# Two down projections by one step of Strassen's algorithm with 512 moving columns, and the exponents of gated attention by one-pass products

## Chip, cores and metric

One core of a Trainium2 chip runs a two-layer transformer trunk in one launch. The metric is the device time of that core in microseconds (us); lower is better.

## What is computed

The trunk runs on 1024 prompt tokens and, with the same weights, on 64 sample tokens (8 sequences of 8), all in float32. Layer 0 mixes by gated linear attention and sparse attention, layer 1 by sliding-window attention with sinks; each is followed by a gated feed-forward block. Cut to what matters here:

```python
def trunk(x, ...):
    for l in range(2):
        mix = even_or_odd_mixing(l, x)
        h = layer_norm(ALPHA * x + mix, ln_g[l, 0], ln_b[l, 0])
        x = layer_norm(ALPHA * h + swiglu(h, ffn_w_gu[l], ffn_w_down[l]), ln_g[l, 1], ln_b[l, 1])

def swiglu(h, w_gu, w_down):          # w_gu 1024 x 5632, w_down 2816 x 1024
    g, u = split(h @ w_gu)
    return (silu(g) * u) @ w_down     # the down projection
```

Gated linear attention works in chunks of tokens. Of each chunk it needs exp(sum of log gates / 16) for many sets of summands; these sums are products of the log gates z (128 tokens x 256 features) with constant 0/1 matrices `sums`.

## The kernel before

**Splits.** Where float32 precision is wanted at one pass of TensorE, an operand is split in two F32R tensors: `hi = round(x)` (ScalarE copy) and `lo = x - hi` (VectorE, or GpSimd in the input projections). A product is then three matmuls: hi hi, lo hi and hi lo. Where a tensor is used as plain F32, TensorE takes each matmul in more passes; the trace has two records for each of them.

**`ffn_up`** (from L2091) makes the gated activations by Strassen-Winograd with moving operands of 272 columns and stores them in DRAM (`a_dram`, 22 blocks of 128 features x 1088 tokens).

**`ffn_down`** (from L2387) computes 1088 tokens x 2816 x 1024 and the second layer norm of the layer, once per layer (tags `ffn0d` and `ffn1d`). The 1024 output columns go in 4 chunks of 256 (`NF`). For chunks 0 to 2 the loop over the 22 feature blocks is outside and the 9 token tiles (8 of 128, one of 64 sample tokens) inside, so that 9 tiles x 3 matmuls use one pair of splits (L2475); all tiles of a chunk accumulate in PSUM, two to a bank. The last chunk goes tile by tile (L2507), so that each tile is finished and normalised while the next is multiplied. The moving operand is always the weight block of 256 columns, the stationary one 128 (or 64) tokens of the activations. In all 4 x 22 x 9 x 3 = 2376 matmuls.

- SyncE (L2435 on) loads weights in a ring of 8 buffers and each activation block `aT[:, k, :]` once.
- ScalarE makes `w_hi` (256 columns) and `a_hi` (1088), L2523 and L2552, in the last chunk groups of up to 1024 columns (L2529).
- VectorE makes `w_lo` (L2593) and `a_lo` (L2616, L2600), adds each chunk to the residual `X` (`add`, L2587), and does the layer norm's statistics, centre and reciprocal (L2049 to L2075).
- GpSimd loads `X` and adds the norm's bias (L2080). It does nothing else in this stage.
- With `XT` given (layer 0) each finished tile is transposed by TensorE (L2491) and copied by ScalarE (L2535) for the next stage.

ScalarE waits for the last activations of `ffn_up` before it starts, since the split buffers take the place of that stage's buffers.

**Gated attention** (second Block of `even_in`) runs beside the last three chunks of the input projection. For each chunk i of 128 tokens (8 prompt chunks, then the samples) there are 8 levels l. The order of TensorE's work is written out by hand: at each level some units of the projection (`LEVEL_UNITS`; 6 matmuls of 256 columns each), at levels 0 to 2 a preparatory step for the next chunk, then `level(i, l)`, and at levels 3 to 7 one of five parts of `exponents(i + 1)` (L698): `z` of 128 features stationary, two of nine `sums` matrices (256 columns) moving, both plain F32. `level(i, l)` waits until VectorE has taken level l - 1 (`take_level`, L1006), and each part of `exponents` until ScalarE has exponentiated the part before (L855). VectorE's order at level 1 is: take the level, `late_scaled(i)` (L997, L998), `clip(i + 1)` (L977), `mean_square`. `qk_transposes` (L707) waits for `clip`. ScalarE at level 1: `gates`, then `inverse_rms` with its reload of the exponential's table, and only then, at level 2, `qk_copies`.

## Time and profile before

| | |
|---|---|
| median of 3 runs | 3362.34 us (3362.22 to 3362.91) |
| the profiled execution | 3366.61 us |
| its span, first to last instruction | 3364.9 us |
| mean granted TensorE clock | 0.942 of full speed |
| TensorE busy with matmuls | 3046.8 us, 91% |
| VectorE, ScalarE, GpSimd busy | 49%, 38%, 23% |
| DMA | 241.14 MB, mean 72 GB/s |

A busy TensorE is not TensorE at its peak: matmuls overlap, so what one costs is the distance from its start to the next one's start, not the duration in its record. The idle time before an instruction stands in brackets with what ended it.

### The profile page before, as it was taken

What the parts mean: (1) busy time and instruction counts of PE and PEld (TensorE: products, weight loads), DVE (VectorE), ACT (ScalarE), POOL (GpSimd) and SP (SyncE); (2) the same over time, 40 slices, a digit from 0 to 9 for tenths busy, and PEclk for the clock granted to TensorE, in tenths of its full rate; (3) what the DMA queues carried; (4) which work ended last, traced back from release to release, by engine and by line L of the source; (5) the groups of instructions that cost most, each with busy time, mean ns of one, the idle gap of its engine ahead of it and who ended that gap; (6) DMA issues with size and microseconds to landing.
All of it is one profiled execution on the core that took longest, in us unless ns stands there. A gap on an engine that the chain in (4) does not pass through costs nothing. (4 is left out here: it accounts for less than half of the span.)

```text
span 3364.9 us, 56085 instructions
## 1 busy us (share of the span) xinstructions
PE 3046.8 (91%) x21594; PEld 2653.5 (79%) x21613; DVE 1648.0 (49%) x3148; ACT 1267.7 (38%) x2701; POOL 759.5 (23%) x917
## 2 busy tenths in 40 slices
PE   7999998678999789999999969869996999999997
PEld 7888776354665489999999869836665999999997
DVE  2166343574898363333355634325546333334566
ACT  2222443333565443333344432114444333333343
POOL 2200221530121034444200014400002444430002
PEclk8999997798999899999999989969998999999999
DMA  4201102533100122222351112130002222217111
GB/s 129 76 27 42 26 26 79 161 87 121 35 30 28 44 66 73 81 77 77 127 174 51 41 57 39 64 109 23 32 20 70 77 78 77 78 53 266 38 54 54
DMA packets 253632, 241.14 MB, mean 72 GB/s; under 512 B 55635, under 2 KB 213542, under 8 KB 253350
## 3 DMA queue, kind: packets, MB, share of 16 engines
q1 hardware_dynamic: 244630, 217.87, 21.1%
q0 software_dynamic: 8752, 19.81, 1.9%
q8 instruction: 172, 2.82, 0.4%
q14 instruction: 78, 0.64, 0.1%
HBM read 183.46 MB, written 55.89 MB: 71 GB/s over the span
## 5 line engine op out<-in xcount | busy, mean ns | idle before, releaser
L2204 PE MATMUL ffn0u_ps<-ffn0u_x_hi,ffn0u_whi 128*128 128x272 f32 x1232 | 359.2, 292 | 19.8 <-DVE ffn0u_wlo L2307 11.1
L2204 PE MATMUL ffn1u_ps<-ffn1u_x_hi,ffn1u_whi 128*128 128x272 f32 x1232 | 358.7, 291 | 19.3 <-DVE ffn1u_wlo L2307 10.8
L2204 PE MATMUL ffn0u_ps<-ffn0u_x_hi,ffn0u_wlo 128*128 128x272 f32 x1232 | 356.7, 290 | 0.0
L2204 PE MATMUL ffn1u_ps<-ffn1u_x_hi,ffn1u_wlo 128*128 128x272 f32 x1232 | 356.6, 289 | 0.0
L221 PE MATMUL ine_ps<-ine_w_hi,ine_x_hi 128*128 128x256 f32 (+2 forms) x864 | 261.2, 302 | 5.1 <-DVE ine_w_lo L237 5.0
L2204 PEld LDWEIGHTS ffn0u_ps<-ffn0u_x_hi,ffn0u_whi 128*128 128x128 f32 x1232 | 234.8, 191 | 22.1 <-DVE ffn0u_wlo L2307 20.6
L2204 PEld LDWEIGHTS ffn1u_ps<-ffn1u_x_hi,ffn1u_whi 128*128 128x128 f32 x1232 | 234.5, 190 | 21.6 <-DVE ffn1u_wlo L2307 20.2
L221 PE MATMUL ine_ps<-ine_w_hi,ine_x_lo 128*128 128x256 f32 (+2 forms) x864 | 245.3, 284 | 0.0
L221 PE MATMUL ine_ps<-ine_w_lo,ine_x_hi 128*128 128x256 f32 (+2 forms) x864 | 244.7, 283 | 0.0
L2204 PEld LDWEIGHTS ffn0u_ps<-ffn0u_x_hi,ffn0u_wlo 128*128 128x128 f32 x1232 | 235.0, 191 | 0.0
L2204 PEld LDWEIGHTS ffn1u_ps<-ffn1u_x_hi,ffn1u_wlo 128*128 128x128 f32 x1232 | 234.6, 190 | 0.0
L2204 PE MATMUL ffn1u_ps<-ffn1u_q,ffn1u_whi 128*128 128x272 f32 x704 | 202.5, 288 | 0.0
L2204 PE MATMUL ffn0u_ps<-ffn0u_q,ffn0u_whi 128*128 128x272 f32 x704 | 202.5, 288 | 0.0
L2475 PE MATMUL ffn1d_ps<-ffn1d_w_hi,ffn1d_a_hi 128*128 128x256 f32 (+1 forms) x594 | 171.1, 288 | 14.9 <-DVE ffn1d_a_lo L2609 7.8
L2475 PE MATMUL ffn0d_ps<-ffn0d_w_hi,ffn0d_a_hi 128*128 128x256 f32 (+1 forms) x594 | 171.2, 288 | 14.6 <-DVE ffn0d_a_lo L2609 7.5
L221 PEld LDWEIGHTS ine_ps<-ine_w_hi,ine_x_hi 128*128 128x128 f32 (+1 forms) x864 | 161.8, 187 | 16.1 <-issue 8.3
L2475 PE MATMUL ffn1d_ps<-ffn1d_w_hi,ffn1d_a_lo 128*128 128x256 f32 (+1 forms) x594 | 170.1, 286 | 0.0
L2475 PE MATMUL ffn1d_ps<-ffn1d_w_lo,ffn1d_a_hi 128*128 128x256 f32 (+1 forms) x594 | 170.0, 286 | 0.0
L2475 PE MATMUL ffn0d_ps<-ffn0d_w_hi,ffn0d_a_lo 128*128 128x256 f32 (+1 forms) x594 | 169.8, 286 | 0.0
L2475 PE MATMUL ffn0d_ps<-ffn0d_w_lo,ffn0d_a_hi 128*128 128x256 f32 (+1 forms) x594 | 169.7, 286 | 0.0
L221 PEld LDWEIGHTS ine_ps<-ine_w_hi,ine_x_lo 128*128 128x128 f32 (+1 forms) x864 | 161.9, 187 | 4.8 <-issue 4.0
L221 PEld LDWEIGHTS ine_ps<-ine_w_lo,ine_x_hi 128*128 128x128 f32 (+1 forms) x864 | 161.9, 187 | 0.0
(537 smaller groups left out, 8279.2 us busy)
## 6 DMA issues: line engine op xcount, KB each, us to landing
aT<-scratch_a SPq DMA_DIRECT2D x42, 544.0 KB, 7.6
ffn0u_raw<-in_ffn_w_gu_dram SPq DMA_DIRECT2D x44, 512.0 KB, 5.2
ffn1u_raw<-in_ffn_w_gu_dram SPq DMA_DIRECT2D x44, 512.0 KB, 5.5
scratch_a<-ffn0u_u SPq DMA_DIRECT2D x44, 272.0 KB, 2.1
scratch_a<-ffn1u_u SPq DMA_DIRECT2D x44, 272.0 KB, 2.1
ffn0d_w<-in_ffn_w_down_dram SPq DMA_DIRECT2D x88, 128.0 KB, 2.5
ffn1d_w<-in_ffn_w_down_dram SPq DMA_DIRECT2D x88, 128.0 KB, 2.5
ine_w<-in_w_in_even_dram SPq DMA_DIRECT2D x5, 1024.0 KB, 5.4
```

Source lines behind the costliest of these rows:

```text
L221: last = nc.tensor.matmul(o, xp[:, k, i * P:i * P + r], wp[:, g % RING, 0:n], start=(k == 0 and j == 0 and i % 2 == 0), stop=(k == KD - 1 ...
L2204: last = nc.tensor.matmul(ps[:, bank + h, 0:TOK2], wp, xp, start=(begins and k == 0 and n == 0), stop=(k == KH - 1 and n == 2), skip_group ...
L2475: last = nc.tensor.matmul(acc(i), ap[:, n % 2, i * P:i * P + rows(i)], wp[:, k, :], start=(k == 0 and j == 0 and i % 2 == 0), stop=(k == K ...
```

## The change

**Down projection.** `ffn_down` is rewritten. Activations A (1024 prompt tokens x 2816) and weights B (2816 x 1024) are each cut in 2 x 2 quadrants; seven products of half-size factors, with 11 feature blocks each, replace eight. In a product each of 11 steps multiplies 4 tiles of 128 tokens with a weight block of 512 columns: 12 matmuls a step. Factors that are sums are made on the way: all 55 sums of weights on GpSimd, and of the 55 sums of activations 37 on GpSimd and 18 on VectorE (`dve_sums_a`), each of 128x512. The splits are now two blocks of 128x512 per step, in rings of 5. The 64 sample tokens ride beside products 0, 1, 4 and 5: their hi and lo parts lie side by side as one stationary operand of 128 columns, so two matmuls a step do, and a `fold` matmul adds the halves. Each product is added to one or two quadrants of `X` by VectorE (`take`, 48 additions of 128x512) at step 3 of the next product. Weights come in a ring of 3 (plus 2 for second summands). The norms of tiles 0 to 3 are made within products 5 and 6, those of the samples and tiles 4 to 7 after the last step's splits; the last three steps of product 6 go tile by tile.

```diff
-def ffn_down(nc, st, A, l, tag, aT, XT, y_out, a_out, place=None):
-    NCH, NB, RAW, AG = D // NF, (TILES + 1) // 2, 8, 8
+def ffn_down(nc, st, A, l, tag, aT, XT, y_out, a_out):
+    KH2, HT, HN, RB, RW, RS, TAIL = KF // 2, SEQ // 2, D // 2, 5, 3, 2, 3
+    FACTOR_A = [(A11,), (A11, ADD, A12), (A11, ADD, A22), (A12, SUB, A22), (A22,), (A21, ADD, A22), (A21, SUB, A11)]
+    FACTOR_B = [(B12, SUB, B22), (B22,), (B11, ADD, B22), (B21, ADD, B22), (B21, SUB, B11), (B11,), (B11, ADD, B12)]
+    INTO = [[(0, 1, ADD), (1, 1, ADD)], [(0, 0, SUB), (0, 1, ADD)], [(0, 0, ADD), (1, 1, ADD)], [(0, 0, ADD)],
+            [(0, 0, ADD), (1, 0, ADD)], [(1, 0, ADD), (1, 1, SUB)], [(1, 1, ADD)]]
+    def dve_sums_a(n):
+        return n in a_sum_at and n in w_sum_at and n % KH2 % 2 == 0
...
             @block.sync
...
+                    if n in raw_at:
+                        r = raw_at[n]
+                        if r >= RW:
+                            sp.wait_ge(w_split, raw_steps[r - RW] + 1)
...
             @block.tensor
...
+                def tile_step(p, k, t):
+                    n = p * KH2 + k
+                    for j, (ap, wp) in enumerate(((a_hi, w_hi), (a_lo, w_hi), (a_hi, w_lo))):
+                        last = nc.tensor.matmul(ps[:, bank(p, t), :], ap[:, n % RB, t * P:t * P + P], wp[:, n % RB, :],
+                                                start=(k == 0 and j == 0), stop=(k == KH2 - 1 and j == 2), skip_group_check=True)
...
             @block.scalar
...
+                def split(n):
+                    if n in w_sum_at:
+                        act.wait_ge(w_sum_done, w_sum_at[n] + 1)
...
+                    if n >= RB:
+                        act.wait_ge(step_done, n - RB + 1)
+                    nc.scalar.copy(w_hi[:, n % RB, :], w_source(n)).then_inc(w_hi_done, 1)
...
+                    nc.scalar.copy(a_hi[:, n % RB, :], a_source(n)).then_inc(a_hi_done, 1)
...
             @block.gpsimd
...
+                for n in range(STEPS):
+                    if n in w_sum_at:
+                        sum_w(pool, nc.gpsimd, n)
+                    if n in a_sum_at and not dve_sums_a(n):
+                        sum_a(pool, nc.gpsimd, n, a_sum_pool)
...
             @block.vector
...
+                for n in range(STEPS):
+                    if n + 1 < STEPS and dve_sums_a(n + 1):
+                        sum_a(dve, nc.vector, n + 1, a_sum_dve)
+                    dve.wait_ge(w_hi_done, n + 1)
+                    nc.vector.tensor_tensor(w_lo[:, n % RB, :], w_source(n), w_hi[:, n % RB, :].bitcast(F32),
                                             ALU.subtract).then_inc(w_split, 1)
+                    dve.wait_ge(a_hi_done, n + 1)
+                    nc.vector.tensor_tensor(a_lo[:, n % RB, :], a_source(n), a_hi[:, n % RB, :].bitcast(F32),
+                                            ALU.subtract).then_inc(a_split, 1)
...
+                    if p >= 1 and k == 3:
+                        take_all(p - 1)
...
+                norm(3)
+                ln.dve_rstd(dve, 3)
+                for i in range(4, NT):
+                    half_stats(i, 0)
+                add_sample(0)
+                norm(NT)
+                ln.dve_rstd(dve, NT)
+                for t in range(4):
+                    take(NPROD - 1, t)
+                    half_stats(4 + t, 1)
+                    ln.dve_center(dve, 4 + t, link)
+                    ln.dve_rstd(dve, 4 + t)
```

`sum_a` waits until the low part of the sum two before it has been made (`RS` = 2).

**Gated attention.** `z` is split too, by two operations of VectorE in `log_gates`; the `sums` are copied to F32R once at the start; each part of `exponents` is now two F32R matmuls (`z_hi`, `z_lo`) for each 128 features in place of one F32 matmul. `late_scaled` moves behind `clip` and `mean_square`. On ScalarE `qk_copies` comes before the reload of the exponential's table. For the samples, the levels are interleaved with the products with the old state, and the last norm is made between the updates of the states.

```diff
-                        which = sums_p[:, a:b, :] if i < NT else sums_s[:, a:b, :]
                         for p in range(2):
-                            last = nc.tensor.matmul(exponents_of(i, a, b)[:, :, p, :], z[0:r, p * P:(p + 1) * P], which,
-                                                    start=True, stop=True)
+                            for part in (z_hi, z_lo):
+                                last = nc.tensor.matmul(exponents_of(i, a, b)[:, :, p, :], part[0:r, p * P:(p + 1) * P], which,
+                                                        start=part is z_hi, stop=part is z_lo)
...
                         if l == 1:
-                            late_scaled(i)
                             clip(i + 1)
                             if i >= 1:
                                 mean_square(i - 1)
+                            late_scaled(i)
```

## Rows read from the trace of the kernel before

**Rows 1.** The page, part 1: busy time, share of the span, instructions.

```profile
PE 3046.8 (91%) x21594; PEld 2653.5 (79%) x21613; DVE 1648.0 (49%) x3148; ACT 1267.7 (38%) x2701; POOL 759.5 (23%) x917
```

**Rows 2.** Lines L2475, L2507: durations ns (min/median/max), first and last start us.

```profile
L2475 PE MATMUL ffn0d_ps<-ffn0d_w_hi,ffn0d_a_hi x594: 277/283/552, 1663.7 to 1891.2; 128*128 128x256 f32 x198
L2475 PE MATMUL ffn1d_ps<-ffn1d_w_hi,ffn1d_a_hi x594: 277/283/553, 3043.6 to 3271.3; 128*128 128x256 f32 x198
...
L2507 PE MATMUL ffn0d_ps<-ffn0d_w_lo,ffn0d_a_hi x198: 276/283/415, 1891.8 to 1992.9; 128*128 128x256 f32 x176, 128*64 128x256 f32 x22
L2507 PE MATMUL ffn1d_ps<-ffn1d_w_lo,ffn1d_a_hi x198: 277/283/283, 3271.9 to 3351.6; 128*128 128x256 f32 x176, 128*64 128x256 f32 x22
```

**Rows 3.** Timeline, PE, 256 columns: start, duration; 24 rows left out.

```profile
3340.51 0.28 PE L2507 MATMUL ffn1d_ps<-ffn1d_w_hi,ffn1d_a_lo 128*128 128x256 f32 x1
...
3343.51 0.28 PE L2507 MATMUL ffn1d_ps<-ffn1d_w_lo,ffn1d_a_hi 128*128 128x256 f32 x1
```

**Rows 4.** Timeline, PEld, before F32 matmuls of 512 columns; 3 rows left out.

```profile
2300.22 0.19 PEld L2989 LDWEIGHTS odd_ps<-odd_w,odd_YT 128*128 128x128 f32 x1 [0.24 <-issue]
...
2301.94 0.19 PEld L2989 LDWEIGHTS odd_ps<-odd_w,odd_YT 128*128 128x128 f32 x1 [0.24 <-issue]
```

**Rows 5.** Timeline of POOL, then DVE, in the up projection.

```profile
2701.77 1.30 POOL L2155 TENSOR_TENSOR ffn1u_wlo_full<-ffn1u_raw,ffn1u_wlo_full 128x512 f32<-128x512 f32 x1
2703.01 1.80 POOL L2155 TENSOR_TENSOR ffn1u_wlo_full<-ffn1u_raw 128x512 f32<-128x512 f32 x1
2704.78 1.74 POOL L2155 TENSOR_TENSOR ffn1u_wlo_full<-ffn1u_raw,ffn1u_wlo_full 128x512 f32<-128x512 f32 x1
...
2702.97 2.39 DVE L2307 TENSOR_TENSOR ffn1u_wlo<-ffn1u_raw,ffn1u_whi 128x512 fp32r<-128x512 f32 x2 [3.51 <-ACT ffn1u_whi L2216]
2705.28 0.77 DVE L2322 TENSOR_TENSOR ffn1u_x<-ffn1u_x,ffn1u_ps 128x272 f32<-128x272 f32 x2
```

**Rows 6.** Groups by line, ACT, 2550 to 3043 us: busy us, mean ns.

```profile
L2216 ACT CAST ffn1u_whi<-ffn1u_wlo_full 128x512 fp32r<-128x512 f32 x88 | 52.4, 617 | 7.9 <-POOL ffn1u_wlo_full L2155 7.9
```

**Rows 7.** Stretches: length, busy PE, PEld, DVE, ACT, POOL, granted clock, DMA share, GB/s.

```profile
1920.00:1950.00 30.00, 23.96 (x168) 23.54 (x168) 14.75 (x25) 9.89 (x14) 4.80 (x2) 0.84 0.09 36
...
3043.00:3070.00 27.00, 26.37 (x198) 26.41 (x199) 12.97 (x17) 11.55 (x17) 0.00 (x0) 0.87 0.99 374
```

**Rows 8.** Timeline, PE: the first matmul of the down projection.

```profile
3043.63 0.55 PE L2475 MATMUL ffn1d_ps<-ffn1d_w_hi,ffn1d_a_hi 128*128 128x256 f32 x1 [7.78 <-DVE ffn1d_a_lo L2609]
```

**Rows 9.** Timeline of DVE, ACT, POOL: the norm of the last tiles, both layers.

```profile
3345.09 0.41 DVE L2587 SCALAR_TENSOR_TENSOR ffn1d_X<-ffn1d_X,ffn1d_ps 128x256 f32<-128x256 f32 x1
...
3346.58 1.28 DVE L2058 SCALAR_TENSOR_TENSOR ffn1d_X<-ffn1d_X,ffn1d_ln_mv,ffn1d_ln_gb 128x1024 f32<-128x1024 f32 x1
3347.77 0.16 DVE L2075 RECIPROCAL ffn1d_ln_rstd<-ffn1d_ln_rstd 128x1 f32<-128x1 f32 x1
...
3354.78 2.19 ACT L2070 ACTIVATE ffn1d_X<-ffn1d_X,ffn1d_ln_rstd 128x1024 f32<-128x1024 f32 x2 [1.12 <-DVE ffn1d_ln_rstd L2075]
...
3356.01 4.64 POOL L2080 TENSOR_TENSOR ffn1d_X<-ffn1d_X,ffn1d_ln_gb 128x1024 f32<-128x1024 f32 x2 [4.37 <-ACT ffn1d_X L2070]
...
2002.83 0.80 ACT L2535 COPY XT_odd<-ffn0d_ps 128x256 f32<-128x256 f32 x2 [0.44 <-PE ffn0d_ps L2491]
```

**Rows 10.** What PE waited for, 325 to 600 us: total, times, longest us.

```profile
PE ine_ps L707 <- DVE gla_z L977: 12.4, 8, 2.4
```

**Rows 11.** Timeline of PE and DVE in gated attention, prompt chunks.

```profile
380.18 1.13 PE L698 MATMUL ine_ps<-gla_sums,gla_z 128*128 128x256 f32 x4
380.96 0.47 PE L221 MATMUL ine_ps<-ine_w_hi,ine_x_hi 128*128 128x256 f32 x1
...
387.66 0.49 PE L747 MATMUL ine_ps<-H,gla_A 128*128 128x128 f32 x2
...
386.83 0.77 DVE L1006 COPY_PREDICATED gla_A<-ine_lev,ine_ps 128x256 f32<-128x256 uint8 x2 [0.93 <-PE ine_ps L727]
...
400.70 1.22 DVE L997 TENSOR_TENSOR gla_E<-gla_E,gla_KQ 128x1024 f32<-128x1024 f32 x1
```

More of the change, by code:

```diff
@@ L793, in _ @@
                 kin_transposes(NT)
-                for l in range(1, lv(NT)):
-                    level(NT, l)
-                pe.wait_ge(lev_used, lev0[NT + 1])
+                level(NT, 1)
                 pe.wait_ge(late_done, NT + 1)
+                pe.wait_ge(late_evac, NB * (NCH - CW))
                 pe.wait_ge(ss_in, 32)
@@ L920, in _ @@
                 kin_copy(NT)
+                log_mean_square(NT - 1)
                 inverse_rms(NT - 1)
@@ L2030, with __init__ @@
 class LayerNorm:
-    def __init__(self, st, ctx, tag, l, which, X, A):
+    def __init__(self, st, ctx, tag, l, which, X, A, order=tuple(range(TILES))):
         nc = st.nc
+        self.pos = {i: n for n, i in enumerate(order)}
         self.nc, self.X = nc, X
@@ L2437, in ffn_down, with sum_a, bank @@
+        def sum_a(eng, op, n, done):
+            u, k = a_sum_at[n], n % KH2
+            x, sign, y = FACTOR_A[n // KH2]
+            wait_block(eng, x, k)
+            wait_block(eng, y, k)
+            if u >= RS:
+                eng.wait_ge(a_split, a_sum_steps[u - RS] + 1)
+            op.tensor_tensor(a_sum[:, u % RS, :], a_block(x, k), a_block(y, k), sign).then_inc(done, 1)
+        def bank(p, t):
+            return (4 * p + t) % 7
         with nc.Block() as block:
@@ L2512, in _ @@
+                for t in range(4):
+                    for k in range(KH2 - TAIL, KH2):
+                        last = tile_step(NPROD - 1, k, t)
+                    last.then_inc(tile_done, 1)
+                    if XT is not None and t < 3:
+                        transposes((2, 3, NT)[t])
                 if XT is not None:
-                    for i in range(TILES - 3, TILES):
+                    for i in range(4, NT):
                         transposes(i)
@@ L2579, in _ @@
+                for i in NORM_ORDER[2:]:
                     ln.pool(pool, i)
@@ new lines, in take @@
+                def take(p, t):
+                    if t < 3 or p == NPROD - 1:
+                        dve.wait_ge(tile_done, 3 * p + t + 1)
+                    else:
+                        dve.wait_ge(step_done, KH2 * (p + 1))
+                    for h, c, sign in INTO[p]:
+                        if p == 0 and h == 0:
+                            dve.wait_ge(*((x_first, 32) if t == 0 else (x_right, 32)))
+                        elif p == 1 and t == 0 and c == 0:
+                            dve.wait_ge(x_left0, 16)
+                        elif p == 4 and t == 0 and h == 1:
+                            dve.wait_ge(x_left1, 16)
+                        add((p, t, h, c), 4 * h + t, c, sign, ps[:, bank(p, t), :])
@@ new lines, in take_all, with add_sample, half_stats, norm @@
+                def take_all(p):
+                    for t in range(4):
+                        take(p, t)
+                def add_sample(c):
+                    dve.wait_ge(s_folded, 2 - c)
+                    if c == 1:
+                        dve.wait_ge(x_sample, 16)
+                    add(("s", c), NT, c, ADD, ps[0:NS, S_BANK, :])
+                def half_stats(i, c):
+                    dve.wait_ge(added, touched[(i, c)])
+                    ln.dve_half_stats(i, c, link)
+                def norm(i):
+                    half_stats(i, 0)
+                    half_stats(i, 1)
+                    ln.dve_center(dve, i, link)
@@ new lines, in sample_lo @@
+                def sample_lo(n, slot, src):
+                    dve.wait_ge(s_hi, n)
+                    nc.vector.tensor_tensor(s_a[:, slot, :, NS:2 * NS], src, s_a[:, slot, :, 0:NS].bitcast(F32),
+                                            ALU.subtract).then_inc(s_lo, 1)
+                nc.vector.tensor_tensor(fold[:, :], st.ident[:, 0:NS], st.ident[:, NS:P], ALU.add).then_inc(fold_made, 1)
+                for n in range(STEPS):
+                    if n + 1 < STEPS and dve_sums_a(n + 1):
+                        sum_a(dve, nc.vector, n + 1, a_sum_dve)
@@ new lines, in _ @@
+                    p, k = divmod(n, KH2)
+                    if n == 0:
+                        sample_lo(1, 0, aT[:, 0:KH2, SEQ:NTOK])
+                    elif n == 8:
+                        for h in range(2):
+                            dve.wait_ge(s_in[h], 16)
+                        nc.vector.tensor_tensor(s_sum[:, :, :], aT[:, 0:KH2, SEQ:NTOK], aT[:, KH2:KF, SEQ:NTOK],
+                                                ALU.add).then_inc(s_summed, 1)
+                    elif n == 10:
+                        sample_lo(2, 1, s_sum[:, :, :])
+                    elif n == 2 * KH2:
+                        sample_lo(3, 0, aT[:, KH2:KF, SEQ:NTOK])
```

538 lines of the change are left out of this document (311 added, 227 removed).

## The prediction

> **What bounds the kernel now.** I read the page's busy times first: TensorE works 91% of the span [rows 1], so a stage gets shorter where its matmuls get fewer or cheaper, as long as what feeds them keeps up. Next, per line, where the down projections lie: their matmuls run from 1663.7 to 1993.2 us in layer 0 and from 3043.6 to 3351.9 us in layer 1 [rows 2], 329.5 and 308.3 us. Then the timeline, for what a matmul costs: 25 steps of 256 columns in 3.00 us, 120 ns each [rows 3]. Here 2376 x 0.120 = 285 us of each projection is plain TensorE work; the other engines have slack. After the last matmul the norm of the last tiles remains: layer 1's span ends at 3364.9, layer 0's last copy at 2003.6 [rows 9]. The two projections so take 321.3 us (3043.6 to 3364.9) and 339.9 us (1663.7 to 2003.6). Layer 0 is slower since its last chunk also transposes tiles and stalls, in part at a granted clock of 0.84 [rows 7].
>
> **1. Price of a 512-column matmul.** The count falls from 2376 x 256 columns to 7 x 11 x 12 = 924 for the prompt and 4 x 11 x 2 = 88 for the samples, 1012 x 512. No F32R matmul of 512 columns is in the trace. 512 columns take 213.3 ns at 2.4 GHz, 256 take 106.7. At 256 the steps are 13 ns longer than the columns [rows 3]; at 512, in plain F32 with two rounds of columns to a record, 4 steps take 1.72 us, 430 ns, only 3 over 2 x 213.3 [rows 4]. So the price lies between 214 and 226 ns. I take 216, the row with the same number of columns, since there too one weight load hides behind twice its own columns. 1012 x 0.216 = 218.6; two folds in F32, two records of 0.43 each, 1.7; start at the lower clock as now, 13% of 27 us [rows 7], 3.5. TensorE alone: **224 us**.
>
> A rule of the Trainium skill (TensorE: Matmul & The Clock Gate, section Back-to-back issue gap) gives N/2.4 + 2.5 ns for an isolated matmul, 215.8 at 512, but names about 131 ns as the sustained figure at N = 512. The same formula gives 109 ns at 256, where this trace has 120; by 131 ns the sum would be 133 us instead of 219.
>
> **2. What feeds it: VectorE and GpSimd take turns.** GpSimd has 55 + 37 = 92 sums of 128x512 per layer, VectorE 154 low parts + 18 sums. The timeline of the up projection shows the two together [rows 5]. Alone, a GpSimd sum is followed by the next after 1.24 us (2701.77 to 2703.01). The next one meets a low part of VectorE and is followed only after 1.77 (to 2704.78), and VectorE's two low parts last 2.39 us. GpSimd and VectorE do not overlap there: one sum and one low part cost 1.24 + 0.53. VectorE's operations with a PSUM operand (0.77 for two, at 2705.28) run beside GpSimd at their usual pace, so the 48 additions of `take` don't count in this. By product:
> - 0, 1, 4, 5: 11 x 1.24 + 22 x 0.53 = 25.3 us, against TensorE's 11 x 14 x 0.216 = 33.3 us. Hidden.
> - 2, 3, 6: 16 x 1.24 + 28 x 0.53 = **34.7 us**, against 11 x 12 x 0.216 = 28.5 us. Not hidden: 6.2 us short each, plus about 1.5 for moments in which neither has work.
>
> The rings give credit. ScalarE may split step n once step n - 5 is done; its two copies take 0.62 each [rows 6], the low part 0.6, so a step is ready 4 x 2.59 - 1.9 = 8.5 us ahead. Products 2 and 3 together need 2 x 7.7 = 15.4, so 7 us of stall. Products 4 and 5 restore the credit (`take_all`, 8 additions of 0.68, 5.4 us in which no low part is made, fits in it; 0.68 is estimated from the 0.41 of 256 columns [rows 9] and 0.27, half of the 0.53 above). Product 6 needs 7.7, and one norm addition on GpSimd (2.3) and a centre (1.2) fall on it: 11.2 - 8.5, some 4 with holes. **11 us** of stalls per layer, and 4 for the clock when TensorE idles in short pieces, of which half the loss seen at 0.84 [rows 7] is my measure (0.16 x 30 = 4.8).
>
> The Trainium skill (SBUF — State Buffer, section SBUF: two separate sides) calls this an exclusive lock on a port pair that both use, held for the whole instruction; it holds for VectorE operations with two SBUF inputs. By that rule, the trace agrees.
>
> **3. Start.** Now the first matmul comes 7.78 us late [rows 8]. The new chain has 512 weight columns, not 256, and a GpSimd sum of 1.24 us before the high part, but that sum waits for nothing of ScalarE. I add 1.
>
> **4. Tail.** The last 36 matmuls (7.8 us) can only begin once the splits of the last step are made, and so does the chain of norms. Per tile of 128 the centre holds the shared turn for 1.2, GpSimd's bias 2.3 (4.64 for two), and they alternate: reciprocal, ScalarE's scale 1.1 (2.19 for two), GpSimd 2.3 to 2.4, centre of the next tile 1.2 [rows 9]. That is 4.8 us per tile, though VectorE's own sequence from addition to reciprocal takes 2.75 (3345.09 to 3347.84) [rows 9]. Chain after the last split: norm of tile 3 (the 2.75 without an addition but with both halves' statistics, 0.7 each by the 1.49 from addition to centre [rows 9]: 3.3), four half statistics and the samples' addition (3.6), the samples' norm (3.2), addition and statistics of tile 4 and its wait for GpSimd's turn with the samples (4.7), four centres at 4.8 distance (14.4), scale, bias and store of the last (1.1 + 2.4 + 4.2, the last from the end of GpSimd at 3360.65 to the end of the span). Sum 37 us for layer 1. In layer 0, 33 to the last bias and 2.3 for transposes and copies.
>
> **5. Sum of the projections.** Layer 1: 1 + 224 + 11 + 4 - 7.8 + 37 = 269.2, against 321.3: -52. Layer 0: 1 + 224 + 15 - 7.8 + 2 (transposes within the stage) + 33 + 2.3 = 269.5, against 339.9: -70. TensorE's own saving of about 60 us is thus partly given back in layer 1 by stalls and a longer tail, while layer 0 also loses its present stalls.
>
> **6. Gated attention.** Four records of `exponents` and the way to the next projection matmul take 380.18 to 380.96 and the 0.19 us that this one starts early (0.47 against 0.28): 0.97 us [rows 11]. Four F32R matmuls of 256 columns are 4 x 0.12 = 0.48. For the parts at levels 3 to 5 that is 1.5 us per chunk. At levels 6 and 7 I count nothing: there TensorE is already level with VectorE's `take_level` (0.77 us from 386.83, the outputs at 387.66) [rows 11], which would be late next. `clip` no longer stands behind `late_scaled`, whose first operation alone lasts 1.22 [rows 11]; TensorE's wait for it is 12.4 us over 8 chunks [rows 10], 1.5 each, and goes. The two new operations of VectorE on `z` (about 0.4 each) make `exponents` wait some 0.3. `qk_copies` a table load earlier is off the path. Net 2.7 x 8 = 21.6, and 2 for the samples' reordering: **-23**. The sums' conversion and two more small tensors hide behind the 16 units of projection at the start.
>
> **Total:** 52 + 70 + 23 = 145 us. The profiled execution took 3366.6 us, 4.3 above the median; off the median 3362.3 the forecast is **3217 us**. A measurement of this kernel can tell about 0.2%, 7 us, from no change.
>
> **The rivals.**
> - *No turn-taking to speak of*: short waits interleave, TensorE is never starved, and the tail goes at VectorE's 2.75 to 3.0 us per tile. Then 2 x (15 + 8) less: 3171. Against it: 1.77 against 1.24 [rows 5].
> - *512 columns at 226 ns*, the excess of [rows 3] kept: 2 x 10 more, of which the stalls absorb a part: 3229 to 3237.
> - *The feed loop is slower than the turns.* With 3 weight buffers, low part to load to GpSimd's sum to high part to low part must go round once in three steps, and a_sum has two buffers. If steps of products 2, 3 and 6 take 3.8 us instead of 3.3: 2 x 33 x 0.5 = 33 more, 3250.
> - *Gated attention gives nothing*, since level and `take_level` alternate anyway: 3240.
> - *The other sign: slower.* Place: VectorE's queue in `ffn_down`. If each of its 172 low parts and sums had to wait for one whole GpSimd operation, 172 x 1.77 + 48 x 0.68 = 337 us per layer in place of 239, so 3217 + 196 = 3413. It decides from 145/2/172 = 0.42 us of extra waiting per operation. Against it: GpSimd has just 92 operations to be waited for.
> - *TensorE stops binding*: matmuls of 512 columns overlap so far that the turns alone set the pace, 4 x 25.3 + 3 x 34.7 = 205 us in place of 239, 34 less per layer: 3149. Nothing in the rows points there; 256 columns already cost 120 ns [rows 3]. The sustained figure of the Trainium skill's TensorE page (above) would lead here.
>
> **Chances.** Forecast 42%, no turn-taking 15%, 226 ns 13%, slower loop 16%, attention nothing 9%, slower 3%, TensorE not binding 2%. The range reaches from the first rival to the third with some room for sums of them: 3172 to 3255. All but one case are faster by over 0.2%: faster 0.96, same 0.01, slower 0.03.
>
> **What would show it.** Right: steps of 216 ns within product 0; in products 2, 3 and 6 steps of about 3.2 us with TensorE waiting for `w_lo` or `a_lo`, GpSimd sums lasting 1.8 where VectorE is busy; last matmul about 22 us (layer 1) before the span's end, against 13 now; no wait at the `qk` transposes. Wrong: TensorE waiting in product 0 or 1 (a DMA or ring bound), or 512-column steps over 230 ns, or GpSimd sums at 1.3 throughout.

## The result, and the profile after it

The changed kernel takes **3269.22 us** (median of 6 runs, 3264.14 to 3282.22), beside 3362.62 us for the kernel before (6 runs, 3361.39 to 3370.67): ratio 0.9722, 95% interval 0.9706 to 0.9737. That is faster, as forecast, but 52 us above the forecast of 3217 and 14 us above the upper end of the range. The profiled execution took 3274.2 us (span 3272.5), 5 above the median.

The page of the changed kernel, part 1 (busy time, share of the span, instructions), answers to [rows 1]:

```profile
PE 2939.8 (90%) x18874; PEld 2460.4 (75%) x18893; DVE 1775.2 (54%) x3186; ACT 1204.3 (37%) x2655; POOL 1040.3 (32%) x1097
```

VectorE has 127 us more to do and GpSimd 281 more; TensorE is busy for 107 less. To find where the time went, I read in both traces when the first matmul of each stage starts and took differences (us):

| part | before | after | difference | predicted |
|---|---|---|---|---|
| input projection with gated attention | 586.5 | 583.0 | -3.5 | -23 |
| the up projection ahead of layer 0's down projection, with the wait at its start | 490.4 | 493.4 | +3.0 | +1 |
| layer 0: its first matmul to the next stage's | 350.3 | 293.2 | -57.1 | -71 |
| the same ahead of layer 1's | 489.9 | 491.9 | +2.0 | +1 |
| layer 1: its first matmul to the end of the span | 321.3 | 285.8 | -35.5 | -53 |
| all other stages | | | -1.2 | 0 |
| sum | | | -92.3 | -145 |

Three parts fall short of the forecast: the attention by 19.5 us, layer 0 by 16 and layer 1 by 18.5, the starts included.

**The matmuls.** Timeline of TensorE in product 2 of layer 1 (start, duration; it answers to [rows 3]):

```profile
3066.21 0.39 PE L2604 MATMUL ffn1d_ps<-ffn1d_w_hi,ffn1d_a_hi 128*128 128x512 f32 x1
...
3069.85 0.39 PE L2604 MATMUL ffn1d_ps<-ffn1d_w_hi,ffn1d_a_lo 128*128 128x512 f32 x1
```

From the first to the second, 16 matmuls start in 3.64 us: 227.5 ns for 512 columns. Over the 213.3 ns (512 / 2.4) that the prediction counts for the columns, the excess is 14 ns, as it was 13 at 256 [rows 3].

**The waits.** What TensorE waited for in layer 1, 2985 to 3273 us (total, times, longest):

```profile
PE ffn1d_ps L2604 <- DVE ffn1d_X L2780: 11.7, 2, 6.5
PE ffn1d_ps L2604 <- DVE ffn1d_a_lo L2828: 10.8, 2, 9.9
PE ffn1d_ps L2604 <- DVE ffn1d_X L2776: 1.9, 1, 1.9
```

The 9.9 is the start (7.8 before [rows 8]). Apart from that, TensorE hardly waits for the low parts, where the prediction had put its stalls. It waits for lines L2780 and L2776, the additions of `take`. The timeline around the longest of these waits, at the change from product 2 to product 3, TensorE first, then VectorE:

```profile
3096.47 0.39 PE L2604 MATMUL ffn1d_ps<-ffn1d_w_lo,ffn1d_a_hi 128*128 128x512 f32 x1
3103.36 0.80 PE L2604 MATMUL ffn1d_ps<-ffn1d_w_hi,ffn1d_a_hi 128*128 128x512 f32 x1 [6.50 <-DVE ffn1d_X L2780]
3103.95 0.63 PE L2604 MATMUL ffn1d_ps<-ffn1d_w_hi,ffn1d_a_lo 128*128 128x512 f32 x1
3104.37 0.63 PE L2604 MATMUL ffn1d_ps<-ffn1d_w_lo,ffn1d_a_hi 128*128 128x512 f32 x1
...
3094.91 1.57 DVE L2825 TENSOR_TENSOR ffn1d_w_lo<-ffn1d_w,ffn1d_w_hi 128x512 fp32r<-128x512 f32 x1
3096.41 1.75 DVE L2828 TENSOR_TENSOR ffn1d_a_lo<-ffn1d_a_sum,ffn1d_a_hi 128x512 fp32r<-128x512 f32 x1
3098.29 1.54 DVE L2533 TENSOR_TENSOR ffn1d_a_sum<-aT 128x512 f32<-128x512 f32 x1
3099.75 1.75 DVE L2825 TENSOR_TENSOR ffn1d_w_lo<-ffn1d_w,ffn1d_w_hi 128x512 fp32r<-128x512 f32 x1
3101.43 0.68 DVE L2828 TENSOR_TENSOR ffn1d_a_lo<-ffn1d_a_sum,ffn1d_a_hi 128x512 fp32r<-128x512 f32 x1
3102.03 4.86 DVE L2780 TENSOR_TENSOR ffn1d_X<-ffn1d_X,ffn1d_ps 128x512 f32<-128x512 f32 x8
```

At 3094.65 TensorE begins step 0 of product 3. Three tiles on, it needs the bank of the fourth, and by `bank(p, t)` (seven banks, L2535) that is the one in which tile 0 of product 2 lies. VectorE clears it in `take_all`, which stands behind the low parts of step 3, and the turns with GpSimd stretch four of the five operations shown before it from 0.68 to 1.5 us and more. TensorE stands for 6.5 us with splits at hand: those of step 2 are ready at 3098.16 and those of step 3 at 3102.11. When it resumes, its pitch is 0.43 us (3103.95 to 3104.37), that of the lower clock. The start times of the steps give the price in layer 1: the first two steps of products 1, 3 and 6 take 2.5 + 1.2, 7.4 + 1.4 and 6.1 + 2.1 us longer than such steps do elsewhere, **21 us**.

What holds VectorE up in product 3 is its own queue of stretched operations, and not a wait for GpSimd's sums or for loads: it is busy for 36.0 of 38.8 us (length; busy us of PE, PEld, DVE, ACT, POOL; granted clock; DMA share; GB/s).

```profile
3094.65:3133.45 38.80, 32.30 (x134) 26.24 (x132) 36.01 (x38) 14.64 (x26) 25.12 (x16) 0.91 0.40 134
```

**The tail** takes as long as predicted. VectorE's centres and GpSimd's shifts for the last tiles, as in [rows 9]:

```profile
3247.21 3.07 DVE L2082 SCALAR_TENSOR_TENSOR ffn1d_X<-ffn1d_X,ffn1d_ln_mv,ffn1d_ln_gb 128x1024 f32<-128x1024 f32 x1
...
3252.02 3.08 DVE L2082 SCALAR_TENSOR_TENSOR ffn1d_X<-ffn1d_X,ffn1d_ln_mv,ffn1d_ln_gb 128x1024 f32<-128x1024 f32 x1
...
3261.31 2.34 POOL L2104 TENSOR_TENSOR ffn1d_X<-ffn1d_X,ffn1d_ln_gb 128x1024 f32<-128x1024 f32 x1 [2.48 <-ACT ffn1d_X L2094]
3266.12 2.34 POOL L2104 TENSOR_TENSOR ffn1d_X<-ffn1d_X,ffn1d_ln_gb 128x1024 f32<-128x1024 f32 x1 [2.47 <-ACT ffn1d_X L2094]
```

4.81 us per tile, and 36.6 us from the last low part (3235.91) to the end of the span; 4.8 and 37 were forecast. The last matmul starts 28.4 us before the end. The prediction's sign for this said 22, but its own sum gives 37 - 7.8 = 29.

**Gated attention.** The wait of the `qk` transposes for `clip` [rows 10] is 2.4 us, once, in place of 12.4:

```profile
PE ine_ps L715 <- DVE gla_z L992: 2.4, 1, 2.4
```

A part of `exponents` is shorter too. From its first matmul to the next projection matmul it took 0.97 us [rows 11]; now it takes 0.58:

```profile
376.59 0.39 PE L706 MATMUL ine_ps<-gla_sums,gla_z_hi 128*128 128x256 f32 x1
...
377.17 0.28 PE L221 MATMUL ine_ps<-ine_w_hi,ine_x_hi 128*64 128x256 f32 x1
```

The stretch from 325 to 550 us, in it most of the chunks (length; busy us of PE, PEld, DVE, ACT, POOL; granted clock; DMA share; GB/s), of the kernel before and of the changed one:

```profile
325.00:550.00 225.00, 205.24 (x1519) 166.50 (x1517) 89.69 (x227) 101.68 (x244) 53.21 (x146) 0.97 0.11 30
```

```profile
325.00:550.00 225.00, 210.91 (x1538) 175.01 (x1538) 97.47 (x245) 101.86 (x246) 55.66 (x146) 0.89 0.13 33
```

TensorE idles less and yet gets on no faster: the granted clock fell from 0.97 to 0.89. An estimate from these rows, as if TensorE had set the pace all the time, is 0.08 x 225 = 18 us, close to the 19.5 that are missing.

### The profile page after: what moved, and what is told of

It is laid out like the page before. It is cut to its first block and busy times, and to the rows that moved or that the text cites. A ratio compares the mean times of both kernels' runs of the same rounds, so it can differ in the third digit from the quotient of the medians.

```text
span 3272.5 us, 50986 instructions
## 1 busy us (share of the span) xinstructions
PE 2939.8 (90%) x18874; PEld 2460.4 (75%) x18893; DVE 1775.2 (54%) x3186; ACT 1204.3 (37%) x2655; POOL 1040.3 (32%) x1097
## 5 line engine op out<-in xcount | busy, mean ns | idle before, releaser
L2228 PE MATMUL ffn0u_ps<-ffn0u_x_hi,ffn0u_whi 128*128 128x272 f32 x1232 | 358.8, 291 | 20.4 <-DVE ffn0u_wlo L2331 10.6
L2228 PE MATMUL ffn0u_ps<-ffn0u_e,ffn0u_whi 128*128 128x272 f32 x528 | 154.7, 293 | 0.0
L2228 PE MATMUL ffn1u_ps<-ffn1u_e,ffn1u_whi 128*128 128x272 f32 x528 | 154.6, 293 | 0.0
L2604 PE MATMUL ffn0d_ps<-ffn0d_w_hi,ffn0d_a_hi 128*128 128x512 f32 x308 | 125.2, 407 | 24.1 <-DVE ffn0d_X L2780 11.7
L2604 PE MATMUL ffn1d_ps<-ffn1d_w_hi,ffn1d_a_hi 128*128 128x512 f32 x308 | 124.5, 404 | 24.4 <-DVE ffn1d_X L2780 11.7
L3343 POOL TENSOR_TENSOR odd_X<-odd_X,odd_gb 128x1024 f32<-128x1024 f32 (+1 forms) x9 | 21.2, 2352 | 358.6 <-ACT odd_X L3304 358.6
L2228 PEld LDWEIGHTS ffn0u_ps<-ffn0u_q,ffn0u_whi 128*128 128x128 f32 x704 | 132.6, 188 | 0.0
```

What stands on the lines that cost most here:

```text
L2228: last = nc.tensor.matmul(ps[:, bank + h, 0:TOK2], wp, xp, start=(begins and k == 0 and n == 0), stop=(k == KH - 1 and n == 2), skip_group ...
L2604: last = nc.tensor.matmul(ps[:, bank(p, t), :], ap[:, n % RB, t * P:t * P + P], wp[:, n % RB, :], start=(k == 0 and j == 0), stop=(k == KH ...
L3343: nc.gpsimd.tensor_tensor(X[0:r, j % 4, :], X[0:r, j % 4, :], gb[0:r, 1, :], ALU.add).then_inc(norm_done, 1)
```

## The experiments

Theory: (A) the bank waits, made long by the turns, and 14 ns per matmul are what the projections lack; (B) in the attention, what lets the clock fall is the one-pass form of the exponents. Rivals are named with each run. "Stage" is the first row of the table above; a layer is counted from its first matmul to the next stage's or the end. Two sizes of chance belong beside every comparison. The runs were made in groups on different chips, and the kernel before, timed with each group, has medians from 3362.6 to 3366.2 us, so times from different groups compare to some 3 us; the ratios take this out. Stages and layers come from one profiled execution of each kernel: five kernels with the same down projections (the changed one, e1, e5, e6, e9) give 292.5 to 297.4 us for layer 0 and 285.8 to 288.0 for layer 1.

**e1, e2: each half alone.** Edits: the diff's hunks in `ffn_down` and `LayerNorm` alone, or the others alone.

> The changed down projections with the attention of the kernel before. My theory from the two traces: the down projections bring 57 us (layer 0) and 36 us (layer 1), the attention stage only a few, so about 3363 - 93 + 4 = 3270 to 3274 us, ratio to before 0.972 to 0.974, the whole of the gain. Rival (my prediction's step 6: the attention part is worth 23 us by itself and something else in the changed kernel hid it): 3285 to 3295 us.

> The changed gated attention with the down projections of the kernel before. My theory (shorter chunks given back by a lower granted clock): 3356 to 3361 us, ratio 0.998 to 1.000, and a mean clock in the attention's chunks of 0.88 to 0.90 against 0.97 before. Rival, the step as predicted: 3340 us, ratio 0.993.

Measured: e1 3281.55 us, ratio 0.9754 [0.9738, 0.9770]; e2 3354.42 us, 0.9971 [0.9959, 0.9984], against 3363.71 for before. So the projections bring 82 us, the attention 9, and with the projections changed too it brings 12 (3281.6 to 3269.2). e1 came out 8 us above what I expected, in part since its layer 0 took 297.4 us against 293.2, and e2 some 2 us below. The attention is worth more in the median than the profiled stage told, but only half of the 23. The clock in e2 from 325 to 550 us is 0.89, in e1 0.98.

**e3: tile 0 taken early.**

```
-                    if p >= 1 and k == 3:
-                        take_all(p - 1)
+                    if p >= 1 and k == {1: 2, 2: 2, 3: 1, 4: 2, 5: 2, 6: 2}[p]:
+                        take(p - 1, 0)
+                    if p >= 1 and k == 3:
+                        for t in range(1, 4):
+                            take(p - 1, t)
```

> The changed kernel, but VectorE takes tile 0 of the last product one or two steps earlier than tiles 1 to 3, since TensorE needs that bank alone at the next product's first step. Theory A (the bank waits of 20 us per layer are a loss of their own): the waits of TensorE for the additions fall from 24.6 to under 8 us per layer, part of it comes back as waits for the splits (the lead of the splits is 3 to 5 us at its least), net 8 to 13 us per layer, so 3269 - 16 to 26 = 3243 to 3253 us. Theory B (the turn-taking of VectorE and GpSimd alone sets the products' time, and a bank wait is only where it shows): the waits move to the splits one for one, 3266 to 3272 us.

Measured: 3256.64 us, 0.9678 [0.9662, 0.9694], 12.6 us less, between the two forecasts and nearer to theory A's. Layers 285.7 and 279.8, 7.5 and 6.0 less. TensorE's waits in layer 1 (2975 to 3257 us):

```profile
PE ffn1d_ps L2604 <- DVE ffn1d_a_lo L2829: 20.7, 7, 10.0
PE ffn1d_ps L2604 <- DVE ffn1d_X L2780: 1.9, 1, 1.9
```

(The 24.6 us of the expectation were those of TensorE's matmuls and of its weight loads for L2780 added up, which is mostly the same idle time counted twice; the matmuls' own were 11.7 + 1.9.) The waits for additions are gone but for 1.9, and 10 us of new waits for low parts stand in their place: seven where there were two. In the steps of product 3, VectorE's lead over TensorE, 4 to 11 us in the changed kernel, now falls to 0.15. So the order of the additions cost 6 to 7.5 us per layer, under theory A's 8 to 13. The rest came back as waits for the splits: VectorE's shortage had shown only at the bank.

**e4: no turns.** GpSimd's sums are cut to 16 columns, which leaves the sums out, and the activations' first block is split where GpSimd would have made the sum.

```
-            op.tensor_tensor(raw[:, slot, :], raw[:, slot, :], second, f[1]).then_inc(w_sum_done, 1)
+            op.tensor_tensor(raw[:, slot, 0:16], raw[:, slot, 0:16], second[:, 0:16], f[1]).then_inc(w_sum_done, 1)
```

> The changed kernel with GpSimd's sums cut to 16 columns, and the first block used where a sum of activations was meant: this leaves the sums out of products 0, 2, 3, 4 and 6. Theory A (turn-taking makes the splits and additions late): VectorE's 512-column operations last 0.68 us throughout, TensorE's waits in the products fall under 5 us per layer apart from the start of 10, a layer takes 10 + 227 + 28 = 265 us (before: 293 and 286), so 3269 - 28 - 21 = 3215 to 3228 us. Theory B (the waits come from the order of the work, whatever its speed): under 10 us less per layer, 3250 us or more.

Measured: 3212.08 us, 0.9546 [0.9530, 0.9562], 3 us below theory A's range; layers 267.4 and 262.4. One of VectorE's groups of low parts (busy us, mean ns of one, idle before), changed kernel and then e4:

```profile
L2828 DVE TENSOR_TENSOR ffn1d_a_lo<-ffn1d_a_sum,ffn1d_a_hi 128x512 fp32r<-128x512 f32 x55 | 65.5, 1190 | 0.3
```

```profile
L2829 DVE TENSOR_TENSOR ffn1d_a_lo<-aT,ffn1d_a_hi 128x512 fp32r<-128x512 f32 x59 | 40.6, 689 | 0.8 <-ACT ffn1d_a_hi L2686 0.8
```

1190 ns become 689, and TensorE's only wait left is the start's:

```profile
PE ffn1d_ps L2605 <- DVE ffn1d_a_lo L2829: 9.8, 1, 9.8
```

`take_all` stands where it stood; without the turns its additions come in time. GpSimd's sums with their turns thus cost 25.8 and 23.4 us per layer. e4 doesn't part the turns from the time of the sums themselves, which stand ahead of the splits; that VectorE was busy for 36.0 of 38.8 us in product 3, largely in stretched operations, speaks for the turns. The order of the additions decides how much of the cost shows (e3: 6 to 7.5 less). The attention's stage took 571.7 us here, with the same code as the changed kernel's 583.0; its clock was 0.94. The edit doesn't touch this stage, and 11 of the 60 us between the two profiled executions lie in it.

**e5, e6: the attention's two edits apart.** e5 has the attention of before, its F32 exponents included, but with `clip` and `mean_square` ahead of `late_scaled`; e6 is the changed kernel with `late_scaled` put back:

```
                         if l == 1:
+                            late_scaled(i)
                             clip(i + 1)
                             if i >= 1:
                                 mean_square(i - 1)
-                            late_scaled(i)
```

> The changed down projections; in the attention of the kernel before, only the clip of the next chunk's gates is moved ahead of the late scaling (the exponents stay F32 products in four passes). Theory A (the one-pass products are what lets the clock fall in the chunks): the wait of the gate products for the clip (12.4 us, 8 times) goes, the granted clock between 320 and 545 us stays near 0.97, and the stage before the sampling is 8 to 12 us shorter than the 585 to 586 us of the runs with the old attention; time 3282 - 10 = 3270 to 3275 us. Theory B (any removed wait is taken back by something else in the chunk, the clock has nothing to do with the products' form): the stage stays within 3 us of 585, 3279 to 3283 us.

> The changed kernel with the late scaling put back ahead of the clip (one-pass exponents kept). Theory A: the clock falls as in the changed kernel (0.85 to 0.92 in most windows of 45 us from 325 on) and the clip wait of about 12 us is back, partly hidden by the shorter exponents: the stage before the sampling 586 to 594 us, time 3272 to 3282 us. Theory B: as the changed kernel plus the clip wait in full, 3281 us; the clock as before, near 0.97.

Measured: e5 3270.32 us, 0.9722 [0.9708, 0.9735]; e6 3277.55 us, 0.9738 [0.9725, 0.9752]. Stages 574.6 and 588.5 (e1: 585.2). The stretch from 325 to 550 us in both:

```profile
325.00:550.00 225.00, 211.25 (x1573) 170.82 (x1571) 93.04 (x244) 106.44 (x259) 57.22 (x151) 0.96 0.16 43
```

```profile
325.00:550.00 225.00, 200.99 (x1526) 166.91 (x1524) 97.64 (x245) 102.59 (x245) 55.70 (x147) 0.93 0.11 29
```

Moving `clip` alone is worth 11.2 us (e1 to e5) and keeps the clock; with it the projections reach the whole kernel's 0.9722. The one-pass exponents, with the smaller moves on ScalarE and for the samples that go with them in both runs, are worth 4 us by the medians alone (e1 to e6) and, once `clip` is moved, 1 (e5 to the changed kernel). Neither can be told from zero: the intervals overlap, and from e1 to e6 the profiled stage even grew from 585.2 to 588.5. In e6 the clock is 0.93 where theory A said 0.85 to 0.92, so with the wait for `clip` back it fell less than in the changed kernel.

**e9: the passes doubled.**

```
-                            for part in (z_hi, z_lo):
+                            for part, start, stop in ((z_hi, True, False), (z_lo, False, True)) * 2:
```

> The changed kernel with each one-pass exponent product issued twice, the second pair writing the same result over the first: eight passes of 256 columns per part instead of four, about 20 us more work for TensorE in the attention, as much as the F32 form of before had. If the clock falls because TensorE has less streaming to do in the chunks, it stays at 0.96 to 1.00 there and the stage before the sampling takes 575 to 582 us, no longer than in the changed kernel (583): time 3262 to 3270 us. If the clock falls for another reason (the one-pass form itself, the run's chance), it stays at 0.83 to 0.92 and the stage takes 597 to 605 us: 3283 to 3290 us.

Measured: 3272.67 us, 0.9718 [0.9703, 0.9733]; the stage 579.8, no longer than the changed kernel's 583.0, with 172 matmuls more (20 us at 0.12). Stage and clock are as the first case has them. The time is 3 us above its range, but the ratio to the kernel before is the changed kernel's.

```profile
325.00:550.00 225.00, 214.30 (x1722) 180.51 (x1720) 99.06 (x252) 104.75 (x256) 55.19 (x146) 0.97 0.15 39
```

The clock is back at 0.97 and pays for the added work. This speaks against the F32R form as such: fewer matmul passes in the chunk is what goes with the fall. By what mechanism they bring it about, no run shows. Over all runs, the granted clock from 325 to 550 us is 0.96 to 0.98 in the seven whose exponents take four passes of F32 or the doubled ones (before, e1, e5, e9, e11, e12, e14), and 0.88 to 0.94 in the nine with one-pass exponents (the changed kernel, e2, e3, e4, e6, e7, e8, e10, e13). That is one execution of each. The granted clock of the whole kernel is on record for every execution, and there the two forms differ by less and come near each other: 0.931 to 0.939 in the six of the changed kernel, 0.937 to 0.940 in the nine of e1 and e5, 0.939 to 0.942 in the four of e9. The profiled one of the changed kernel, at 0.932, is among the lowest, so its 0.89 is probably lower than what is usual.

**e7: all activation sums of products 2, 3 and 6 on VectorE**, with e3's early take. Edit: `dve_sums_a` without its `n % KH2 % 2 == 0`.

> The early take of tile 0 (as in the run first_take, 3256.6 us), and in the products with both sums VectorE adds all the activation blocks, not every second one, so that GpSimd has one sum a step. By 1.24 + 0.53 us of turns per step the splits of such a product cost 11 x 2 x 1.24 + 11 x 0.53 + takes = 31 us in place of 35, against TensorE's 30: theory A says 3 to 5 us less of split waits in products 3 and 6 each, 10 to 14 us in the two layers, 3243 to 3248 us. Rival (the sum on VectorE costs it as much as the turn it spares): 3254 to 3262 us.

Measured: 3253.58 us, 0.9666 [0.9651, 0.9681]; layers 289.0 and 278.4 against e3's 285.7 and 279.8. From step 39 to 41, in product 3, a step takes 3.13 us, against the 12 x 0.2275 = 2.73 of TensorE, so the turns still bind and the layers together don't gain; the median's 3 us come with an attention stage that is 4.7 us shorter. The rival's range begins at 3254 and holds within half a us, in this arrangement.

**e8: the tail on VectorE.** For tiles 4 to 7 one VectorE instruction replaces ScalarE's scale and GpSimd's shift:

```
+    def dve_scale_shift(self, dve, i):
...
+        self.nc.vector.scalar_tensor_tensor(out=x, in0=x, scalar=self.rstd[0:r, i, :], in1=self.gb[0:r, 1, :],
+                                            op0=ALU.mult, op1=ALU.add).then_inc(self.norm_done, 1)
```

> The changed kernel, but for the last four tiles VectorE scales and shifts itself in one instruction (1.27 us) where ScalarE scaled (1.15) and GpSimd shifted (2.34). Theory A (the tail is a chain of VectorE, which waits 1.8 us per tile for GpSimd's turn, and ends with ScalarE, GpSimd and a store): per tile 4.81 becomes 4.1 to 4.2 us and the last hop of 3.5 us goes, so 6 us per layer where the end of layer 0 matters as much, 3269 - 9 to 12 = 3257 to 3260 us; layer 1 alone 6 us. Rival (VectorE is full, the instruction that it takes over costs it 1.27 us per tile and the turns stay): within 2 us of 3269.

Measured: 3264.39 us, 0.9694 [0.9679, 0.9709] (4 runs, 3257.15 to 3274.78). The attention's stage, untouched, was 5 us longer in the profiled run, so I read the layers: 288.8 and 283.4, 4.4 and 2.4 less, and from the last matmul to the end 24.9 us against 28.4. The layers' gains are hardly larger than the spread named above; the 3.5 us of the tail are, since e1, e5, e6, e9 and e10 all have 28.4 there within 0.1. Centres now follow each other in 4.39 us and last 1.27, as no shift is met:

```profile
3257.54 1.27 DVE L2082 SCALAR_TENSOR_TENSOR ffn1d_X<-ffn1d_X,ffn1d_ln_mv,ffn1d_ln_gb 128x1024 f32<-128x1024 f32 x1
...
3261.93 1.27 DVE L2082 SCALAR_TENSOR_TENSOR ffn1d_X<-ffn1d_X,ffn1d_ln_mv,ffn1d_ln_gb 128x1024 f32<-128x1024 f32 x1
```

The layers give a little over half of the 6 us expected, and the median is 4 us above the range. The first centre still meets the samples' shift (3.07 us), and VectorE's extra instruction lies in its own queue.

**e10, e13: the 14 ns per matmul.** e10 puts the two products with a_hi side by side; e13 multiplies the upper 16 bits of each factor as BF16 in the tile steps and leaves the low bits out (`x[:, n % RB, :].bitcast(BF16)`, every second element).

```
-                    for j, (ap, wp) in enumerate(((a_hi, w_hi), (a_lo, w_hi), (a_hi, w_lo))):
+                    for j, (ap, wp) in enumerate(((a_hi, w_hi), (a_hi, w_lo), (a_lo, w_hi))):
```

> The changed kernel with the three products of a tile step in another order, so that the two which share the left factor a_hi follow each other. If the 14 us in a thousand (227.5 ns a matmul of 512 columns where 512 at full clock are 213) is the reloading of the left factor, the mean pitch falls to about 223 ns and a layer by 4 us: 3260 us. If it goes with every matmul whatever it loads: pitch 227.5 ns, 3266 to 3272 us.

> The changed kernel with the tile steps of the down projections multiplying the upper 16 bits of each split factor as BF16 (three BF16 products in place of three F32R ones, read at every second 16-bit place; the low bits are left out). If the excess goes with the F32R form: the pitch of a 512-column matmul is 216 ns or less, 924 x 11.5 ns = 10 us less of TensorE work per layer, part of it lost to the feed, so a layer 5 to 10 us shorter (281 and 288 after the step table of the changed kernel, 286 and 293). If it goes with every matmul: 227.5 ns, layers within 3 us of 286 and 293.

Measured: e10 3264.60 us, 0.9696 [0.9681, 0.9710]; its stretch of two sample and twelve tile matmuls lasts 3.20 us, 229 ns each, as in the changed kernel (3.19, 228). e13 3259.50 us (2 runs), 0.9688 [0.9668, 0.9708]; 18 steps of BF16 take 4.08 us, 226.7 ns (one record among them is missing):

```profile
3059.71 0.39 PE L2607 MATMUL ffn1d_ps<-ffn1d_w_hi,ffn1d_a_hi 128*128 128x512 bf16 x1
...
3063.79 0.39 PE L2607 MATMUL ffn1d_ps<-ffn1d_w_hi,ffn1d_a_hi 128*128 128x512 bf16 x1
```

Layers 291.8 and 284.5, within 2 us of the changed kernel's. Neither the new order nor the 16-bit form removes the excess: on these rows it goes with every matmul. e10's time lies between its two cases, and its pitch decides for the second. But e10 doesn't show that loading the left factor is free: layer 1 has 1016 records of weight loads beside 1016 of matmuls in it, as in the changed kernel, so the repeated factor was loaded again. e13 says more on this. Its weight loads are recorded with half the duration of the changed kernel's (the changed one first), and the pitch is the same to 1 ns:

```profile
3068.04 0.19 PEld L2604 LDWEIGHTS ffn1d_ps<-ffn1d_w_hi,ffn1d_a_hi 128*128 128x128 f32 x1
```

```profile
3059.71 0.10 PEld L2607 LDWEIGHTS ffn1d_ps<-ffn1d_w_hi,ffn1d_a_lo 128*128 128x128 bf16 x1
```

So the excess doesn't follow the length of the load. BF16 operands without gaps between their elements weren't tried. The 10 us by which e13's median is lower lie in the attention's stage (572.0, against 583.0), not in the projections.

**e11, e12, e14: a version of what paid.** e11 joins e3, e5 and e8. e12 takes tiles 1 to 3 at steps 3, 5 and 7:

```
-                    if p >= 1 and k == 3:
-                        for t in range(1, 4):
-                            take(p - 1, t)
+                    if p >= 1 and k in (3, 5, 7):
+                        take(p - 1, (k - 1) // 2)
```

e14 adds e7's edit to e12.

> A version of the pieces that paid: the changed down projections with the early take of tile 0 and the tail's scale and shift on VectorE, and the F32 attention with only the clip moved ahead. If the pieces add up (e5 3270, less 13.5 for the take by its stages, less 8 for the tail): 3246 to 3251 us. If the freed tail or take meets another wait in layer 0, where the next stage takes over the tiles: 3254 to 3260 us.

> As e11, and tiles 1 to 3 are taken at the steps 3, 5 and 7 of the next product in place of all at 3. Theory A (a ring of five steps cannot hold the burst of additions, so TensorE waits 3 to 5 us for the splits at step 4 of products 3 and 6 although VectorE catches up later): 2 to 4 us less per layer, 3240 to 3246 us. Theory B (VectorE is short over the whole product and it does not matter where the additions stand): within 2 us of e11.

> As e12, and VectorE adds all the activation blocks of products 2, 3 and 6. In e7 a step of these products took 3.12 us against 2.72 for TensorE and it paid nothing with the additions in one burst (layer 0 3 us longer, layer 1 1.4 us shorter than e3). If the burst was what spoiled it: 2 to 4 us less per layer than e12, 3233 to 3238 us. If the turns cost the same whoever adds: 3239 to 3245 us.

Measured: e11 3245.52 us, 0.9641 [0.9628, 0.9655]; e12 3241.12 us, 0.9630 [0.9617, 0.9643]; e14 **3236.45 us**, 0.9622 [0.9609, 0.9635]. The layers, as a table with the change's own:

| | changed | e3 | e11 | e12 | e14 | e4 |
|---|---|---|---|---|---|---|
| layer 0 | 293.2 | 285.7 | 285.8 | 280.9 | 279.8 | 267.4 |
| layer 1 | 285.8 | 279.8 | 276.7 | 273.8 | 269.3 | 262.4 |

The pieces add up. Spreading the additions gives 4.9 and 2.9 us per layer and 4 in the median, so the bursts of up to six additions look like a loss of their own. Once they are spread, e7's edit gives 1.1 and 4.5 us, in the median 5 and by the ratios 3. The times are as both expectations' first cases have them, and the two layers together shrink by 7.8 and then by 5.6 us. But the intervals of e11, e12 and e14 overlap, and some of the gains per layer are within the spread named above. e14 beats both kernels, by 33 us the changed one. e4, without the sums and with the old tail, is still 12.4 and 6.9 us faster per layer: about that much the sums and their turns still cost.

## Why the forecast was 52 us low

Point by point, by the steps of the prediction:

- **Step 1, the price of a matmul: wrong in size.** 227.5 ns, not 216. 1012 x 11.5 ns = 11.6 us per layer, 23 in all. Of the two rows between which I chose, the 256-column F32R row (13 ns of excess) was the nearer, and the F32 row (3 ns), which I took because its column count was the same, was the wrong one: there, one record has two rounds of columns behind it. e10 and e13 show that the excess depends on neither the order of the left factors nor F32R. The Trainium skill (TensorE: Matmul & The Clock Gate, section Back-to-back issue gap) gives the formula that agreed with my 216 for an isolated matmul, and about 131 ns for a sustained stream at N = 512. Back to back, this kernel shows neither: 227.5 ns.
- **Step 2, the turns: right; where they bind: wrong.** The step failed at "`take_all`... fits in it". Low parts and sums do take turns (e4: 1190 to 689 ns), and e4 prices sums and turns together at 25.8 and 23.4 us per layer. I weighed VectorE's work against the ring of five splits alone and never asked which PSUM bank step 0 of the next product needs, and behind what in VectorE's queue its release stands. Predicted were 11 + 4 us of stalls at the splits, measured 21 at the banks, 5 of them at the lower clock. The 4 for the clock didn't follow from the estimate given for it, half of 4.8, but came out near. e3 shows that some 7 of the 21 were the order's own. The exclusive lock of the Trainium skill (SBUF — State Buffer, section SBUF: two separate sides), which holds for VectorE operations with two SBUF inputs, agrees with the durations: VectorE's additions, with one input in PSUM, last 0.66 to 0.68 us throughout.
- **Step 3, the start: 3.0 and 2.0 us** where 1 was counted. Small.
- **Step 4, the tail: right**, 4.81 us per tile and 36.6 in all; e8 shows the chain by shortening it. In layer 0 the last copy ends 35.3 us after the last low part, as forecast (33 + 2.3).
- **Step 5:** layer 1 came to -33.5 with its start instead of -52, layer 0 to -54.1 instead of -70. In layer 1 the matmul's price explains 11.6 of the 18.5, the stalls 6 and the start 1. In layer 0 the same terms would make 20 where 16 are missing. Two counts went better there: the 2 us for transposes within the stage don't show (its steps run over by as much as layer 1's, 27.7 and 27.3 us in all), and the next stage's first matmul follows the last copy after 9.1 us where it was 10.3.
- **Step 6, the attention: failed at "-23".** `clip`'s wait was worth what I said: 1.5 x 8 = 12 predicted, 11.2 measured (e5). Of the exponents' 1.5 us per chunk some 1.2 came, as shorter work: 0.58 us for a part, not 0.48, saves 0.39 three times. That was taken back by the clock: 0.89 for 0.97. The step priced matmuls at a constant clock, though [rows 7] had shown that it is not given. e9 is the test: 20 us of added matmuls cost nothing. Between the medians (e1 to the changed kernel) the attention gives 12.3 us, 11 short of the 23; in the profiled run, one of the slower ones, 19.5 are missing.
- **The rivals.** "512 columns at 226 ns" came true, "attention gives nothing" in part, and each was priced alone; 3217 + 2 x 11.6 + 11 makes 3251, and the stalls and starts add the rest. The range took in one at a time. The slower feed loop is not what bound: GpSimd did wait for weight loads, 10.6 us in product 3, but VectorE behind it was idle for just 2.8 of 38.8 us.

Open are what makes up the 14 ns, what links fewer matmul passes to a lower clock, and why a stage with the same code takes 571.7 in one run and 583.0 in another: its clock differs (0.94, 0.89), but nothing here shows what decides it.

## What to carry to other kernels

When an engine is fed through a ring and drained through banks, write down for each first use of a bank which instruction frees it and what stands before that in its engine's queue; the ring's credit doesn't help there. Release the one bank that is needed next early, and spread the others. Before making matmuls cheaper in a stage with short waits, look at the granted clock beside it: work that is taken away may come back as a lower clock. Here the edit that removed a wait paid (11 us), and the cheaper matmuls didn't pay measurably.

## What the hardware showed that I had not expected

- 512-column matmuls back to back cost 227.5 ns in F32R and 226.7 in BF16 (e13), and the sample ones with a 64-column left factor no less: 13 to 14 ns over the columns, as at 256 [rows 3]. A weight load recorded with 0.10 us in place of 0.19 changes nothing in this.
- With the same busy time of TensorE in the same 225 us (211.25 us in e5, 210.91 in the changed kernel) the granted clock was 0.96 with the F32 exponents and 0.89 with the one-pass ones; doubling the passes (e9) restored 0.97. The busy share doesn't tell them apart. Each of these clocks is from one execution.
- A VectorE operation of 0.68 us lasts 1.5 to 1.8 when it meets a GpSimd one of the same width, and a centre of 1.27 lasts 3.07 when it meets a shift of 2.34: the waiting is inside the duration, so it shows in no list of waits.
